# The opening of a two-group trunk step: shift and scale in two groups of columns

## What is computed

```
mod = silu(cvec) @ w_mod[l] + b_mod[l]        # six rows of 1024: shift, scale, gate, shift, scale, gate
h = rmsnorm(x, g0) * (1 + mod[1]) + mod[0]
u = h @ w_in[l]                               # 1024 -> 9216: inputs of three token mixers and their gates
m = mixers(u) ... @ w_br, gated, @ w_o        # retention, neighbourhood attention, gated linear recurrence
x = x + mod[2] * rmsnorm(m, g1)
h = rmsnorm(x, g2) * (1 + mod[4]) + mod[3]
f = swiglu(h) in layer 0, two of eight experts in layer 1
x = x + mod[5] * rmsnorm(f, g3)
```

## Time and profile before

| What | Value |
|---|---|
| Median of three runs | 1630.82 us |
| Profiled execution: span, first to last instruction (the profile gives no other time for it) | 1628.5 us |
| TensorE busy | 1559.0 us, 96% |
| DVE, ACT, POOL busy | 1009.0, 809.5, 131.4 us |
| Mean granted clock of TensorE | 0.989 |
| Slab 0's product, the first work of TensorE | at 9.13 us |
| Panel 0's first matmul | at 37.59 us |
| First transfer that POOL issues behind slab 3's product, and its bias | at 31.30 and 34.19 us |

### The profile page before, as it was taken

How to read it: one execution, slowest core, us unless ns; L and a number is a source line. 1 busy time by engine, 2 the same in 40 slices (tenths; PEclk the granted TensorE clock), 3 DMA queues, 4 the chain that set the end, 5 groups by cost and what they waited for, 6 DMA issues and landing times.

```text
span 1628.5 us, 22233 instructions
## 1 busy us (share of the span) xinstructions
PE 1559.0 (96%) x9080; PEld 1192.4 (73%) x9080; DVE 1009.0 (62%) x990; ACT 809.5 (50%) x945; POOL 131.4 (8%) x89
## 2 busy tenths in 40 slices
PE   4999999999999999999989899999999999999997
PEld 1778888777778767888877786677777666766776
DVE  2654699655444665559966875555555556556576
ACT  4533744454333553364445665555545554455465
POOL 2100144000000020013410000000000000000000
PEclk7999999999999999999999999999999999999999
DMA  9875444378774367644435699999999999999991
GB/s 394 325 301 198 167 167 185 120 284 300 288 279 164 131 269 277 227 156 161 186 134 194 241 335 401 406 385 414 399 355 379 418 412 408 398 410 407 401 417 64
DMA packets 56280, 470.36 MB, mean 289 GB/s; under 512 B 6465, under 2 KB 6577, under 8 KB 9073
## 3 DMA queue, kind: packets, MB, share of 16 engines
q1 hardware_dynamic: 53712, 461.27, 72.7%
q0 software_dynamic: 2464, 7.63, 1.2%
HBM read 464.68 MB, written 4.19 MB: 288 GB/s over the span
## 4 chain that ended last, share of the span: by engine, by line
PE 84%; ACT 5%; DVE 5%; DMA 3%; issue 2%; POOL 0%; POOLq 0%; DVEq 0%; ACTq 0%; SPq 0%
PE ps L1313 22%; PE ps L1315 21%; PE ps L1314 21%; PE ps L1787 5%; PE ps L1805 3%; DVE ring_lo L2408 3%; ACT w_hi L977 2%; PE ps L1282 2%; PE ps L1522 1%; DMA ring<-in_w_in 1%; PE ps L1389 1%; PE ps L1424 1%; PE ps L1766 1%; DMA out<-state_out 1%; DMA ring<-in_w_mod 1%
## 5 line engine op out<-in xcount | busy, mean ns | idle before, releaser
L2408 DVE TENSOR_TENSOR ring_lo<-ring,w_hi 128x2048 fp32r<-128x2048 f32 x197 | 449.9, 2289 | 168.8 <-ACT w_hi L977 168.5
L1313 PE MATMUL ps<-ring_lo,h_both 128*128 128x512 f32 x1032 | 410.8, 398 | 0.9 <-DVE ring_lo L2323 0.6
L977 ACT ACTIVATE w_hi<-ring 128x2048 fp32r<-128x2048 f32 x197 | 375.2, 1910 | 68.9 <-PE ps L1315 64.8
L934 ACT ACTIVATE ring_lo<-ring 128x2048 fp32r<-128x2048 f32 x90 | 172.3, 1915 | 159.1 <-PE ps L1315 149.0
L2323 DVE TENSOR_TENSOR ring_lo<-ring,ring_lo 128x2048 fp32r<-128x2048 f32 x74 | 169.0, 2289 | 117.8 <-ACT ring_lo L934 117.2
L1313 PEld LDWEIGHTS ps<-ring_lo,h_both 128*128 128x128 f32 x1032 | 194.2, 188 | 50.4 <-issue 9.8
L1315 PE MATMUL ps<-ring_lo,h_both 128*128 128x512 f32 x592 | 230.8, 390 | 0.0
L1314 PE MATMUL ps<-ring_lo,h_both 128*128 128x512 f32 x592 | 230.5, 389 | 0.0
L1315 PE MATMUL ps<-w_hi,h_both 128*128 128x512 f32 x440 | 172.5, 392 | 0.0
L1314 PE MATMUL ps<-w_hi,h_both 128*128 128x512 f32 x440 | 171.9, 391 | 0.0
L1313 PE MATMUL ps<-ring_lo,act_hi 128*128 128x512 f32 x308 | 125.4, 407 | 9.1 <-DVE ring_lo L2408 7.4
(11 more groups left out here) (389 smaller groups left out, 1990.7 us busy)
## 6 DMA issues: line engine op xcount, KB each, us to landing
ring<-in_w_ff SPq DMA_DIRECT2D x297, 1024.0 KB, 7.4
ring<-in_w_in SPq DMA_DIRECT2D x36, 2048.0 KB, 8.7
u<-in_w_mod SPq DMA_DIRECT2D x21, 2048.0 KB, 9.1
ring<-in_w_br SPq DMA_DIRECT2D x6, 2048.0 KB, 8.5
ring<-in_w_o SPq DMA_DIRECT2D x4, 2048.0 KB, 7.9
ring<-in_w_mod SPq DMA_DIRECT2D x3, 2048.0 KB, 16.7
out<-state_out POOLq DMA_DIRECT2D x4, 512.0 KB, 5.8
x_sb<-in_x SPq DMA_DIRECT2D x1, 1024.0 KB, 10.5
```

Of the source, the lines that this page charges most:

```text
L934: A(hi, ring[s][:, half * UNIT:(half + 1) * UNIT], ACT.Copy).then_inc(mix_hi, 1)
L977: A(part_hi(p, n), ring[slab_slot(n)][:, p * UNIT:(p + 1) * UNIT], ACT.Copy).then_inc(hi_ready[p], 1)
L1313: mm(out, a_hi, b_lo, start=start, stop=False, skip_group_check=True)
L2408: V.tensor_tensor(ring_lo[slot][:, part], ring[slot][:, part], part_hi(p, n).bitcast(F32), ALU.subtract)\
```

## The change

Slabs are put in two groups for the opening: (0, 2) holds shift and scale of columns 0 to 511, (1, 3) those of columns 512 to 1023. In the new order slab 0 and slab 1 are the first group, slabs 2 and 3 the second. Later groups move by one number. The transfers are issued in the order slab 0, x, the first 260 columns of the constants, slab 1, first half of panel 0, slab 2, first half of panel 1, slab 3, the rest of the constants, second halves of panels 0 and 1. Each of the two panels now comes in two transfers.

The units of panels 0 and 1 are split in the order 0, 2, 1, 3. TensorE multiplies slabs 0 and 1, makes the first four blocks of both groups ready, and multiplies the first halves of panels 0 and 1 between the products of slabs 2 and 3. Behind the second shift and scale come the second halves of both panels. The product of slab 4 and that of slab 5 stand behind panel 1. The gate tables of ACT and DVE move behind the split of unit 2. Every use of the rest of the constants in the decay tables waits for the second transfer.

```
-MOD_GROUPS = [mod_slabs(0, 0, 2), mod_slabs(0, 2, 5), ...]
+MOD_GROUPS = [[(0, 0), (0, 2)], [(0, 1), (0, 3)], mod_slabs(0, 2, 5), ...]
-MIX_GROUP, FFN_GROUP = (1, 3), 2
+MIX_GROUP, FFN_GROUP = (2, 4), 3
+FIRST_UNITS = [0, 2, 1, 3]
...
# SP
+            def load_half(j, half):
+                s, _, before = plan["win", 0, j]
+                if half == 0:
+                    sp.wait_ge(*released(before))
+                else:
+                    sp.wait_ge(*slab_loaded(("win", 0, j), 0))
+                part = slice(half * UNIT, (half + 1) * UNIT)
+                sp.dma_start(ring[s][:, part], w_in[0, j][:, part]).then_inc(slab_in[s], 16)
+
+            def start():
+                load(("mod",) + MOD_ORDER[0])
+                sp.dma_start(x_sb, x).then_inc(s_x, 16)
+                sp.dma_start(con[:, 0:NFIRST], consts[:, 0:NFIRST]).then_inc(s_tables, 16)
+                load(("mod",) + MOD_ORDER[1])
+                load_half(0, 0)
+                load(("mod",) + MOD_ORDER[2])
+                load_half(1, 0)
+                load_mod(SLOTS)
+                sp.wait_ge(s_tables, 16)
+                sp.dma_start(con[:, NFIRST:NCONST], consts[:, NFIRST:NCONST]).then_inc(s_tables, 16)
+                for j in range(2):
+                    load_half(j, 1)
+            start()
-                for key in layer_slabs(l):
+                for key in layer_slabs(l)[0 if l else SLOTS + 2:]:
...
# POOL
-                    pool.wait_ge(mod_done, MOD_FROM[1])
+                    pool.wait_ge(mod_done, MOD_FROM[2])
...
# ACT (first_read, first_hi: four blocks at a time, group 0; rounding of both groups)
                     mix_split(0, 0)
-                act.wait_ge(mod_ready, l + 1)
-                turn_read(l, 0, (0,))
-                input_hi(l, 0, (0,))
...
+                    act.wait_ge(mod_ready, 1)
+                    act.wait_ge(xt_half, 1)
+                    first_read(0)
+                    first_hi(0)
+                    mix_split(0, 2)
+                    gate_tables()
+                    copy_mod(1, ps[:, 4:5, :])
+                    mix_split(0, 1)
+                    act.wait_ge(mod_ready, 2)
+                    act.wait_ge(xt_done, 1)
+                    first_read(1)
+                    first_hi(1)
...
                 decay_tables(l)
...
# PE
+            def first_half(j, half, g):
+                key, _, hi, count = mix_unit(0, 2 * j + half)
+                lo = ring_lo[plan[key][0]][:, half * UNIT:(half + 1) * UNIT]
+                hi, lo = (v.rearrange("p (k c) -> p k c", k=4) for v in (hi, lo))
+                ins = by_pass(ps[:, 2 * j + g, :], (h_hi, h_lo), g, 4 * half, hi, lo, (mix_hi, count + 1),
+                              mix_lo_made(0, 2 * j + half), input_made(0, 0, g, half), half == 0, half == 1)
+                if g == 1:
+                    ins.then_inc((mix_half, win_done)[half], 1)
+
+            def start():
+                for q in range(2):
+                    modulate(q, 0, (0,), 0)
+                turn_rows(0, 0, (0,))
+                turn_mod(0, 2, 0)
+                turn_rows(0, 0, (1,))
+                pe.wait_ge(mod_ready, 1)
+                for g in range(2):
+                    first_half(0, 0, g)
+                pe.wait_ge(ht_act, 1)
+                modulate(2, 1, (4,), 0)
+                first_half(1, 0, 0)
+                modulate(3, 1, (4,), 0)
+                first_half(1, 0, 1)
+                pe.wait_ge(ht_dve, 1)
+                turn_mod(1, 6, 0)
+                for j in range(2):
+                    for g in range(2):
+                        first_half(j, 1, g)
...
+            start()
             for l in range(L):
-                first_panel(l)
+                if l:
+                    first_panel(l)
                 for j in range(NWIN):
-                    if j:
+                    if j > 1 - l:
                         panel(l, j)
                     pieces(l, j)
                     if (j > 0 or l == 0) and j < len(MOD_GROUPS[MIX_GROUP[l]]):
...
# DVE (first_modulation: shift and scale of four blocks; first_read: group 1; first_lo: one group, four blocks)
                     link(read_mod(0, 2, 0))
-                    modulation(0, 0, 2, mod_ready, 1)
...
+                    first_modulation(0)
                     mix_split(0, 0)
+                    dve.wait_ge(xt_half, 2)
+                    first_read(0)
+                    first_lo(0, 0)
+                    first_lo(0, 1)
+                    mix_split(0, 2)
+                    gate_tables()
+                    link(read_mod(1, 6, 0))
+                    first_modulation(1)
+                    mix_split(0, 1)
+                    first_lo(1, 0)
+                    dve.wait_ge(xt_done, 2)
+                    first_read(1)
+                    first_lo(1, 1)
...
                 decay_tables(l)
```

More of the change, by code:

```diff
@@ L52 @@
 GATHER_LIGHT, REST, RESTORE = 3, (3, 28), NFS * E - 2
-CONST_W = {"ident": P, "cos": HD, "sin": HD, "above": P, "below": P, "mask_above": P, "mask_below": P,
-           "ramp_up": P, "ramp_down": P, "window": P, "iota": 2 * P, "half": 2, "age": 2, "before": P, "ones": P}
+CONST_W = {"ident": P, "half": 2, "age": 2, "ones": P, "cos": HD, "sin": HD, "above": P, "below": P, "mask_above": P, "mask_below": P,
+           "ramp_up": P, "ramp_down": P, "window": P, "iota": 2 * P, "before": P}
 CONST_AT = {}
@@ L139, with unit_place, unit_at @@
 STEP = {key[0:1] + key[2:]: c for c, key in enumerate(MIX_SLABS[0])}
+FIRST_UNITS = [0, 2, 1, 3]
+def unit_place(l, m):
+    return FIRST_UNITS.index(m) if l == 0 and m < len(FIRST_UNITS) else m
+def unit_at(l, place):
+    return FIRST_UNITS[place] if l == 0 and place < len(FIRST_UNITS) else place
 POOL_UNITS = [2 * c + 4 for c in range(STEP["win", 10], STEP["win", 15] + 2)]
@@ L471, in input_count @@
         def input_count(l, n, g, half):
+            if l == 0 and n == 0:
+                return 2 * half + g + 1
             return 2 * (4 * l + n + g) + half + 1
@@ L483, in summed, with slab_loaded @@
             return ((first_sum, l + 1), (sum_done, 1) if l else (down_done, NFS))[g]
+        def slab_loaded(key, half=1):
+            s, u, _ = plan[key]
+            return slab_in[s], 16 * (u + 1 + (half and s < 2 and key[0] != "mod"))
         def columns(half):
@@ L514, in mix_lo_made @@
                 return mix_lo_pool, len(POOL_UNITS) * l + POOL_UNITS.index(m) + 1
-            return mix_lo, (MIX_UNITS - len(POOL_UNITS)) * l + m + 1 - sum(v < m for v in POOL_UNITS)
+            return mix_lo, (MIX_UNITS - len(POOL_UNITS)) * l + unit_place(l, m) + 1 - sum(v < m for v in POOL_UNITS)
         def mix_used(l, m):
             key, half, _, count = mix_unit(l, m)
+            if l == 0 and m in (0, 2):
+                return mix_half, m // 2 + 1
             return released(key) if half else (mix_half, count // 2 + 1)
@@ L796, in _, with gate_tables @@
             A(cond_pad[:, :, COND_PAD:COND_PAD + 2], cond, ACT.Silu).then_inc(cond_ready, 1)
[L797 to L806, removed]
+            def gate_tables():
+                act.wait_ge(s_const, 16 * 5)
+                act.wait_ge(s_tables, 16)
+                act.wait_ge(gate_in, 1)
+                A(lbw[:, 1:3, :], lbw[:, 1:3, :], ACT.Exp).then_inc(gate_exp, 1)
+                act.wait_ge(gate_in, 2)
+                link(A(lgw[:, 0, :], lgw[:, 0, :], ACT.Exp, scale=-1.0))
+                A(lgw[:, 0, :], lgw[:, 0, :], ACT.Ln, bias=con_("ones")[:, 0:1]).then_inc(gate_exp, 1)
+                act.wait_ge(gate_in, 3)
+                A(kd, kd, ACT.Exp).then_inc(gate_exp, 1)
             def squares_x(l, n, g):
@@ L838, in turn_read, with first_read, first_hi @@
                     ins.then_inc(ht_act, 1)
+            def first_read(half):
+                for k in range(4 * half, 4 * half + 4):
+                    ins = A(h32[:, 0, k, :], ps[:, 4 + half, (k % 4) * P:(k % 4 + 1) * P], ACT.Identity,
+                            scale=modc[:, 1, k, 0:1], bias=modc[:, 0, k, 0:1])
+                ins.then_inc(ht_act, 1)
+            def first_hi(half):
+                blocks = slice(4 * half, 4 * half + 4)
+                for g, read in ((0, ht_act), (1, ht_dve)):
+                    act.wait_ge(read, half + 1)
+                    A(h_hi[:, g, blocks], h32[:, g, blocks], ACT.Copy).then_inc(h_hi_ready, 1)
             def read_gates(l, n, g):
@@ L923, in mix_split @@
                 s, u, _ = plan[key]
-                act.wait_ge(slab_in[s], 16 * (u + 1))
+                place = unit_place(l, m)
+                act.wait_ge(*slab_loaded(key, 0 if l == 0 and m in (0, 2) else 1))
                 if m == MIX_UNITS - 3:
@@ L1293, in turn_mod @@
                 else:
[L1294 removed]
+                    pe.wait_ge(mod_copied, (0, 1, *MIX_GROUP).index(group) + 1)
                 pe.wait_ge(strips_ready, 1)
@@ L2120, in _ @@
[L2120 to L2127, removed]
```

103 lines of the change are left out of this document (60 added, 43 removed).

## The result

The changed kernel takes 1642.54 us (median of five runs, 1640.90 to 1645.35); the kernel before, in the same session, 1629.03. The ratio is 1.0078, 95% interval 1.0067 to 1.0090: by it the change costs 12.7 us (the two medians lie 13.5 apart). The forecast was 1640.2, 9.4 us over the kernel before, with a range of 1635 to 1645. The profiled execution has a span of 1640.3 in place of 1628.5.

The account below looks back on a forecast made before the run. The early stretch was taken as paced by transfers, then TensorE as always busy. Panels done at 62, slab 5's wait and its half-clock product put panel 2 9.4 us later: span 1637.9, plus 2.3 gives 1640.2, range 1635 to 1645.

Parts of the forecast that it names:

- the late bound of the main case: Opening up to panel 2: one more clock loss and a slower slab, panel 2 at 78.5, 12.7 us later, span 1643.5.
- The judge and what follows panel 2: Panel 2's start, 65.80 before, judges the change; its lateness reaches the span's end, and what follows costs nothing.
- Transfers, first shift and scale: Start of the opening: slab 1 lands 1.8 us earlier, at 17.0; first shift and scale ready at 23.4.
- ACT and DVE, the gate tables and TensorE's row: First halves: tables end at 38.7, just hidden under TensorE's row ending 40.4 to 41.9; second shift and scale 42.2 to 43.7.
- The rule of the Trainium skill on a table switch: Gate tables on ACT: about 1.28 us plus 1.38 of draining per switch, ACT's copy at about 43.4, sum up about 2.
- The second halves: Behind the second shift and scale: unit 3 waits for 4.68 us of exponentials, split by DVE at 56.7 to 58.2.
- T: Time when panels 0 and 1 are both done: 61.2 to 62.8, taken as 62; named sign 60 to 64.
- The slab behind: Behind both panels: slab 5 issued only after slab 4's product, stall of 6.7 us, product 3.64, panel 2 at 75.2.
- A: Rival: TensorE never stands between second shift and scale and panel 2, which starts 5.8 us earlier, span 1625.0; chance 0.08.
- B: Rival: only one of the two new stalls before panel 2, +0.8 or +1.0 us, about 1631.7; chance 0.07.
- C: Rival: POOL's later transfers bring DVE's bias late, near 60 at slowest, both panels 4.7 us later, 1644.9; chance 0.08.
- D: Rival: clock stays low in gaps between first halves, two losses of 1.5 us delay everything by 3, 1643.2; chance 0.07.

Follow-up runs that it names:

- f1: Changed kernel with the turn of the second group's rows ahead of the last first-half product of panel 1: 1644.75 us, ratio 1.0090 to the kernel before.
- g4: Changed kernel with the gate tables of ACT and DVE moved early, behind the norm of x: 1646.27 us, ratio 1.0100 to the kernel before.
- e1: Changed kernel with the product of slab 4 moved ahead of panel 1's second halves: 1630.69 us, ratio 1.0005 to the kernel before.
- e4: Kernel before with only the product of slab 4 moved behind panel 1: 1639.94 us, ratio 1.0056 to the kernel before.
- f3: Changed kernel with 28 products of no use in TensorE's stall ahead of slab 5's product: 1638.27 us, ratio 1.0053 to the kernel before.
- f2: Changed kernel with the edits of e3 and f1, and slab 5's product ahead of panel 0's turn: 1630.83 us, ratio 1.0004 to the kernel before.
- e2: Changed kernel with unit 3 split ahead of the decay tables on ACT and DVE: 1636.25 us, ratio 1.0036 to the kernel before.
- f5: f2 with the products of slabs 2 and 3 one behind the other, ahead of panel 1's first half: 1626.38 us, ratio 0.9979 to the kernel before.
- g1: f5 with 12 products of no use in the stall ahead of slab 5's product: 1625.18 us, ratio 0.9971 to the kernel before.
- e3: Changed kernel with the edits of e1 and e2 together: 1629.32 us, ratio 0.9994 to the kernel before.

## Why the prediction was right

The path was right and the forecast loss was too small: 9.4, where 12.07 were measured at panel 2 and 12.7 in the time, the late bound of the main case. That the time came out only 2.3 above the forecast is in part luck, since the kernel before ran 1.8 below the median that the forecast started from.

*The judge and what follows panel 2.* Panel 2's lateness, 12.07, reached the end of the span as 11.8. Panel 3's weights landed at 79.1 (77 forecast) and stopped nothing.

*Transfers, first shift and scale.* Slab 1's product began at 17.08 (17.0 forecast), the first half product at 25.89 (25.7).

*ACT and DVE, the gate tables and TensorE's row.* The tables ended at 39.0 (38.7), the turn ran at 41.30 (40.4 to 41.9), the second shift and scale were ready at 42.9 (42.2 to 43.7). That the tables just hide was right: f1 shows TensorE's row as the holder, g4 that taking them away from there gains nothing. The rule of the Trainium skill on a table switch (ScalarE: Activation LUTs, section What ACT_TABLE_LOAD costs) would have had the copy at 43.4; it ran from 38.67 to 39.25, so no such drain shows here.

*The second halves.* DVE had unit 3 at 57.4 (56.7 to 58.2). Here is the one large term that was mis-sized: what is left of two half products I took at full clock, 4.55 us, so that both panels end at T = 62; it took 7.1, to 64.57, just outside the 60 to 64 that I had named as a sign. I had put a clock loss into the late bound only, though TensorE stood 1.9, worked 1.1, and stood 1.9 again. e1 shows that it was the clock: with the product of slab 4 in that gap the same stretch takes 4.7 at a granted clock of 1.00.

*The slab behind.* Issued 0.1 after the product, landed 7.7 later (7.6), stall 6.78 (6.7), product 3.57 (3.64). e1 takes the stall away by an earlier product alone, e4 makes the same stall in the kernel before, f3 shows its 1.7 of clock. The rule of the Trainium skill that the prediction sets beside this term (DMA: Bandwidth & Descriptors, section Anatomy of one DMA) is fitted on transfers that GpSimd issues, and SP issues this one; the estimate by it, 6.8, is 0.9 short of the 7.7 measured here.

The sum, from 75.2 to 77.87: 2.5 of clock at unit 3 and 0.2 of transfer. It adds up at panel 2, but behind it something was left out: panel 2's own first matmuls were at half clock too (0.80 and 0.63 us where 0.50 and 0.39 stood before), which makes 12.9 at the copy in layer 0.

*The rivals.* A (TensorE never stands) was wrong in the changed kernel, and f2 shows that even with the order mended the transfers set the pace. B: e2 keeps the slab's stall and is 6.7 late at panel 2, not 1.0: its panels end at 58.2 and not 55.4, slab 5 lands after 8.7 and the clock is lost; e1 keeps unit 3's wait and is at 65.07, sooner than the 66.6 that I had. C: the bias landed at 54.2 (12.5 after its issue at 41.69) and was added at 54.42 without a wait, so C failed by 0.2 us only; in f1, where the second rows came sooner, DVE did wait 0.39 for it. D: the first halves, from 25.89 to 41.30, ran at a granted clock of 1.00; the loss came behind them.

## What to carry to other kernels

Where one buffer's next transfer waits for the product that empties it, that product's place sets when the transfer starts: work moved ahead of it takes the cover away from the transfer behind. Look which load each moved instruction releases, and keep it at least one transfer's time ahead of the next use. And look at what the work done early waits for next. In these runs the time fell below the kernel before only in f5 and g1, in which the engines that feed the second halves do their splits before their tables, TensorE makes these halves without a stop, and the transfers behind the opening are issued 3 us sooner; e3 and f2, which lack the last, came out level. A gap that the reordering opens can also cost clock in the matmuls behind it, as at unit 3.

## What the runs showed of the hardware

Behind two stops of 1.9 us with 1.1 us of matmuls between them, the matmuls ran at 1.2 GHz from 57.5 until about 62 and lost 2.5 us; three other runs with two stops there lost as much, within 0.4 us (f1, f3, g4). In e1, where a 1.9 us product stood in the first of the two gaps, the clock stayed at 2.4 GHz behind the second, though it was as long (1.92). Products of no use in a stall were worth 1.7 us in f3 (the product behind them took 1.9 in place of 3.6), and panel 2's first two matmuls took 0.50 and 0.40 in place of 0.80 and 0.63; in g1 they were worth 1.3 (1.9 in place of 3.2).

A slab of 2 MB landed 7.6 to 7.7 us after its issue when no earlier slab or panel was under way (changed kernel, e1, e3, e4), but 8.7 in e2; with panel 2's weights still coming in for another 1.3, 1.4 and 2.2 us it took 8.9 (f5), 8.8 (g1) and 10.2 (f2). And from the first copy of the retention's state to the end, code that no edit touches, the twelve profiled executions took 1486.0 to 1489.7 us.
